# Decoder step on one core: v tiles beside the convolution taps, paired 64-row index scores between v tiles

## What is computed

```python
z = rms_norm(x, norm_g) @ w_in              # q, k, v, gates, index q (8 heads x 64), index k (64), index w (8), GLU
u = glu_a * sigmoid(glu_b)                  # then causal depthwise convolution of width 31 over u
s = einsum('thd,ld->thl', qi, ki) * 64**-0.5
score = einsum('th,thl->tl', wi * 8**-0.5, relu(s)); score = where(k_pos <= q_pos, score, -inf)
_, idx = top_k(score, 256)                  # the 256 best keys of each row are attended
```

## Time and profile before

| | us |
|---|---|
| median of 3 runs | 1038.33 |
| lowest and highest | 1038.2, 1040.77 |
| the profiled execution | 1040.58 |
| its span from first to last instruction | 1038.8 |
| PE busy | 930.8 (90%) |
| DVE busy | 694.0 (67%) |
| ACT busy | 372.5 (36%) |

### The profile page before, as it was taken

How to read it: one execution, slowest core, us unless ns; L and a number is a source line. 1 busy time by engine, 2 the same in 40 slices (tenths; PEclk the granted TensorE clock), 3 DMA queues, 4 the chain that set the end, 5 groups by cost and what they waited for, 6 DMA issues and landing times.

```text
span 1038.8 us, 11317 instructions
## 1 busy us (share of the span) xinstructions
PE 930.8 (90%) x3900; PEld 514.4 (50%) x3900; DVE 694.0 (67%) x1598; ACT 372.5 (36%) x830; POOL 85.4 (8%) x90
## 2 busy tenths in 40 slices
PE   3999999936899999999998899697598789999998
PEld 2866666713243444666643334353366555445432
DVE  5309987999896765888878889966487565432111
ACT  6310101102666656889700000122765364221000
POOL 0211010000541000000000000001011101310000
PEclk9999999877999999999999899788699789999999
DMA  8363020200662302001030000005012102320211
GB/s 291 108 188 62 1 81 3 83 0 1 203 210 83 112 34 84 26 22 61 0 102 21 21 20 12 0 1 210 21 52 61 31 11 62 104 100 31 71 62 42
DMA packets 35314, 69.82 MB, mean 67 GB/s; under 512 B 9609, under 2 KB 11953, under 8 KB 35249
## 3 DMA queue, kind: packets, MB, share of 16 engines
q1 hardware_dynamic: 28089, 43.93, 13.0%
q0 software_dynamic: 7168, 25.17, 7.4%
HBM read 58.46 MB, written 11.11 MB: 67 GB/s over the span
## 4 chain that ended last, share of the span: by engine, by line
PE 72%; DVE 21%; ACT 3%; issue 3%; DMA 1%; SPq 1%; DVEq 0%; ACTq 0%
PE ps L491 67%; DVE ctmp L1267 8%; PE ps L494 4%; DVE ct L1241 1%; DMA xn<-in_x_prompt 1%; DVE pv L1469 1%; ACT PTs L942 1%; ACT uT L1120 1%; DVE LB L1470 1%; DVE mcum L1395 0%; DVE zN L1493 0%; ACT relu L1058 0%; DVE pv L1435 0%; DVE uT L1675 0%; ACT sqj L955 0%
## 5 line engine op out<-in xcount | busy, mean ns | idle before, releaser
L491 PE MATMUL ps<-xT,W 128*128 128x344 f32 x960 | 283.8, 458 | 0.0
L491 PEld LDWEIGHTS ps<-xT,W 128*128 128x128 f32 x960 | 184.0, 193 | 97.6 <-issue 5.6
L491 PE MATMUL ps<-W,xT 128*128 128x512 f32 (+3 forms) x576 | 214.7, 531 | 1.2 <-ACT relu L1058 1.2
L1267 DVE SCALAR_TENSOR_TENSOR ctmp<-uT,chw,ctmp 128x1024 f32<-128x1024 f32 x116 | 152.0, 1310 | 4.1
L491 PEld LDWEIGHTS ps<-W,xT 128*128 128x128 f32 (+1 forms) x576 | 94.9, 185 | 113.7 <-issue 113.3
L1088 ACT ACTIVATE sgj<-SC,candn 128x1024 bf16<-128x1024 f32 (+3 forms) x128 | 114.5, 897 | 8.8 <-DVE candn L1373 6.6
L942 ACT ACTIVATE PTs<-ps 128x512 f32<-128x512 f32 (+3 forms) x96 | 43.1, 484 | 125.7 <-PE ps L494 125.7
L1706 DVE TENSOR_TENSOR ps<-ps,TP 128x256 f32<-128x256 f32 (+1 forms) x64 | 26.4, 412 | 71.2 <-PE ps L491 70.8
L1133 ACT ACTIVATE nsq<-ps 128x512 f32<-128x512 f32 (+1 forms) x18 | 10.7, 596 | 164.5 <-DVE nss L1482 120.9
L491 PE MATMUL ps<-kiT,qz 128*128 128x512 f32 (+3 forms) x160 | 61.7, 530 | 7.6 <-ACT relu L1058 6.5
L494 PE MATMUL ps<-Cc,Pm 128*128 128x128 f32 x288 | 46.6, 303 | 17.7 <-ACT PTs L942 17.5
(11 more groups left out here) (308 smaller groups left out, 1046.4 us busy)
## 6 DMA issues: line engine op xcount, KB each, us to landing
W<-in_w_in SPq DMA_DIRECT2D x8, 2048.0 KB, 8.7
xn<-in_x_prompt SPq DMA_DIRECT2D x8, 512.0 KB, 8.2
W<-in_w_out SPq DMA_DIRECT2D x1, 4096.0 KB, 13.3
resid<-in_x_prompt SPq DMA_DIRECT2D x16, 256.0 KB
out<-resid SPq DMA_DIRECT2D x16, 256.0 KB
out<-V SPq DMA_DIRECT2D x8, 256.0 KB
out<-zN SPq DMA_DIRECT2D x8, 256.0 KB, 2.0
bias_rows<-tprow SPq DMA_DIRECT2D x1, 1536.0 KB
```

The lines of the kernel that those rows point to most:

```text
L491: return nc.tensor.matmul(out, lhsT, rhs, start=start, stop=stop)
L1267: ins = vec.scalar_tensor_tensor(conv[:, c, :] if j == CW - 1 else acc_, src, chw[:, c, j:j + 1], acc_, ALU.mult, ALU.add)
```

## The change

1. `own_score` on PE moves from the tenth qi piece to behind the first v tile. On DVE the own score's operations move ahead by 16 taps, and line 1300 comes 12 taps after them. `decode_u` moves back by 12 taps.
2. The 48 steps become 40 chunks of up to 512 keys and two heads (80 units). PE multiplies rows 0 to 63 and rows 64 to 127 straight from qiT and kiT into two banks (b2 to b5 by turns); `qz` and its copies go. relu has four buffers of 512, in the place of TP, whose load moves in SPq to after the last chunk.
3. The 8 full v tiles are made before the search: five beside the taps (with cached turns 0 and 1), three in slots 5 to 7, each with some ten chunks and two cached turns, half of the chunks in the middle of the tile. The last block's 8 chunks (slot 8) and the sample rows' v tile come last. ACT drains them there, so the search's rounds drain only ga and gc.
4. The cached scores use one bank (b6), and the 1 x 1 matmul (line 638) behind each turn goes. The second sc16 buffer lies where the last block's scores go, so DVE waits in front of that block for the last score DMA (`scd_out[1]`).

```diff
+    CHUNKS = [(i, hp, a) for i in range(2, NT) for hp in range(H // 2) for a in range(0, (i + 1) * P, 512)]
+    FIRST_SLOT, SLOTS = 5, NT + 1
+    CACHED_AT = {1: (0,), 4: (1,), 5: (2, 3), 6: (4, 5), 7: (6, 7)}
+    EVACUATED_EARLY = NT + 1
     def evacuated_after(r):
-        return min(len(DURING_SEARCH), (r + 1) * 33 // 32)
+        return min(len(DURING_SEARCH), EVACUATED_EARLY + r + 1)
@@ PE
-            if j == 9:
-                own_score()
+        def index_scores(n):
+            i, hp, a = CHUNKS[n]
...
+            for e in range(2):
+                begin(("ix", n, e), f"b{2 + 2 * (n % 2) + e}")
+            for e in range(2):
+                r = slice(64 * e, 64 * e + 64)
+                mm(pt(("ix", n, e))[:, 0:width(n)], qiT[r, hp, i * P:(i + 1) * P], kiT[r, a:a + width(n)]).then_inc(plan.fill_sem(("ix", n, e)), 1)
+        for s in range(SLOTS):
+            one, two = halves(s)
...
+            if s < NT:
+                natural("v", s, 2, between)
+            else:
+                between()
+            if s == 0:
+                own_score()
+            for n in cached_in(s)[:1]:
+                cached(n)
+            for n in two:
+                index_scores(n)
+            for n in cached_in(s)[1:]:
+                cached(n)
+        natural("v", NT, 2)
@@ ACT
+        def index_relu(n):
+            for e in range(2):
...
+                if u >= 4:
+                    act.wait_ge(relu_used, u - 3)
@@ DVE
-        taps(0, CW + 24)
+        taps(0, 2 * CW + 5)
...
-        taps(CW + 24, NTAP - 12)
+        taps(2 * CW + 5, NTAP - 28)
...
+        taps(NTAP - 28, NTAP - 16)
         v.wait_ge(*plan.full("sn"))
...
-        taps(NTAP - 12, NTAP)
+        taps(NTAP - 16, NTAP - 8)
+        cached_turn(1)
+        taps(NTAP - 8, NTAP)
+            if (i, hp, a) == (NT - 1, 0, 0):
+                v.wait_ge(scd_out[1], 128)
```

More of the change, by code:

```diff
@@ L526, in natural @@
             rows = P if t < NT else NB
-            o = begin(("z", g, t), f"b{ring[0] % 4}")
+            o = begin(("z", g, t), f"b{ring[0] % banks}")
             ring[0] += 1
             for k in range(KC):
+                if between and k == KC // 2:
+                    between()
                 last = mm(o[0:rows, 0:n], xT[:, k, t * P:t * P + rows], W[:, gi % 2, k, 0:n], k == 0, k == KC - 1)
@@ L1080, in evacuate @@
                 piece_out(g, m, gcT[:, m // 3, a:a + n], sT[:, 3], ACT.Silu)
-        ev = 0
+        for s in range(SLOTS):
+            one, two = halves(s)
+            for n in one:
+                index_relu(n)
+            if s < NT:
+                evacuate("v", s)
+            for n in cached_in(s)[:1]:
+                cached_out(n)
+            for n in two:
+                index_relu(n)
+            for n in cached_in(s)[1:]:
+                cached_out(n)
+        evacuate("v", NT)
+        ev = EVACUATED_EARLY
         for r in range(BITS + 1):
@@ L1777, in _ @@
         for i in range(2, NT):
-            g.wait_ge(relu_used, (i - 1) * H)
+            g.wait_ge(relu_used, 2 * sum(1 for x in CHUNKS if x[0] <= i))
             d = sc(i)[:, i * P:(i + 1) * P]
```

136 lines of the change are left out of this document (63 added, 73 removed).

## The result

The changed kernel takes **1032.87 us** (median of 7 runs) where the kernel before, run beside it on the same chip, takes 1040.77: a ratio of 0.9923, 95% interval 0.9897 to 0.9948. It is faster by 7.9 us, under 1%, and a ratio of 1 lies outside the interval. The forecast was 12.3 us faster, from a median of 1038.33. The profiled execution took 1031.74 us with a span of 1029.9; the forecast's span would have been 1038.8 - 12.3 = 1026.5.

A forecast was written before the change was run, and what follows sets the result against it. PE was taken to bound 346.40 to 547.37 us, nearly tied with DVE. Line 1410 starts 13.3 us earlier, less 1.0 for PE's clock: 12.3 us faster, 1038.33 to 1026.0 us; range 1018 to 1037, own forecast 1018 to 1031.

The forecast's parts named there:

- the case 1031 to 1035.2: Whole kernel: partly lower clock or longer waits would leave the time at 1031 to 1035.2 us; chance 0.13.
- a search that starts after 365 us: Start of the search, forecast near 358 us; a start after 365 us was named as showing the forecast wrong.
- Which engine bounds the search, and the ties there: Search: without v tiles thirty rounds take 4.59 us each, and line 1410 starts directly behind the first norm, 13.3 us earlier.
- The taps: Ahead of the index stage: the 8.11 us glua wait goes (gain 8.1), an own-score wait of 6.1 comes; net 2.7 us.
- When the next turn may start: Index stage, ahead of turn 2: DVE waits for PE's reads of cached turn 1, 258.3 to 262.4 us (4.1 us).
- Small waits for PE at the cached turns add about 1.1: Blocks 2 to 6, turns 3 to 7: waits for PE add about 1.1 us to 68.0; block 6 ends at 338.8.
- The last score DMA: Ahead of the last block: DVE waits 5.5 us, until 344.3, for the last score DMA, which takes 4.8 us.
- The clock loss behind the search: Behind the search: PE's idle of 30 us lowers its clock and costs at most another 1 us.
- first rival: Index scores: pairs don't overlap, index stage 12.7 us later, result 1038.7; chance 0.11 shared with waits that eat the gain.
- The second rival: Blocks from slot 5: PE at 1.2 GHz gives 1043.8 us (slower: 0.09, shared); a third of blocks costs 5 to 8.
- The rounds did shorten: Search, rival: ACT's counts and drains set the first ten rounds, 19.5 us gain missing, 1045; slower 0.09, shared.
- waits that eat the gain: Index stage: waits use up the gain, time within 1035.2 to 1041.4 us; chance 0.11, shared with pairs in series.

The follow-up runs named there:

- e2: Changed kernel with all nine v tiles put back behind the index scores and drained in the search's rounds: 1036.64 us, ratio 0.9966 to the kernel before.
- e9: Changed kernel with the chunks of blocks 2 to 6 spread from slot 4 instead of 5, cached turns rearranged: 1021.08 us, ratio 0.9867 to the kernel before.
- e3: Changed kernel with only the decode u operation back at its old place, 12 taps sooner: 1032.64 us, ratio 0.9925 to the kernel before.
- e6: Changed kernel with DVE's second cached turn of slots 5 to 7 put behind three chunks of the second half: 1036.78 us, ratio 0.9969 to before.
- e4: Changed kernel with PE making the own score ahead of the first v tile: 1032.95 us, ratio 0.9959 to the kernel before.
- e1: Changed kernel with each pair of index matmuls done twice into the same bank: 1041.44 us, ratio 1.0011 to the kernel before.
- e10: Changed kernel with the edits of e9 and e7 together: 1020.15 us, ratio 0.9791 to the kernel before.
- e11: Changed kernel with the edits of e9, e7 and e4 together: 1017.03 us, ratio 0.9760 to the kernel before.
- e5: Changed kernel with the second sc16 buffer in the KV buffer, so DVE skips the last score DMA's wait: 1033.96 us, ratio 0.9915 to before.
- e7: Changed kernel with ACT draining the sample rows' v tile after round 0's counts: 1034.22 us, ratio 0.9944 to the kernel before.
- e12: The same code as e9, measured again: 1020.46 us, ratio 0.9802 to the kernel before.

## Why the prediction was right, and where it was off

*How right.* The 7.9 us lie inside the stated range (1018 to 1037), but not inside what the prediction called its own forecast, 1018 to 1031: it is the case 1031 to 1035.2, to which it gave 0.13. One of its own signs of being wrong came true, a search that starts after 365 us (365.57). And the number was helped by something that no term foresaw: the stretch behind the choice operation was 2.4 us shorter than before, where the sum had it 1.0 longer. That is luck; with the sum's own figure for that stretch the kernel would have taken about 1035 us, still inside the range.

*Which engine bounds the search, and the ties there: right.* Rounds of 4.60 us on average, PE's idle time of 29.3 us behind it, and the choice operation directly behind the norm came as written. From the first candidate to the last it took 138.1 us (forecast 139.4), from there to the choice operation 29.6 (29.9). The table load fell into round 1 (378.30 - 373.19 = 5.1 us) and cost 0.5 us of the 0.75 foreseen. e2 takes the v tiles back and brings back the slow rounds and the wait for PE. What it does not bear out is the size: the sum booked the whole gain to the search, and e2 has 5.4 of the 6.5 us at the choice operation with v where it was. The sum has no term for that: it never asks when PE's chain would start with the paired scores alone. Whether e9's 12 us need v where the change puts it, no run shows either.

*The taps: right in place, sizes off, without effect.* The decode u wait went. The own score's wait was 3.83 us, not 6.1: DVE came to it at 228.1 and not at 226.4 (1.1 of it because its first tap began at 80.17 and not at 79.03), PE's answer at 231.9 and not at 232.5. The first weighing began at 269.33, forecast 269.7, because PE's row, which the forecast had right to 0.4 us, sets it. e3 shows that this, and not the taps, is the reason: with the 8.11 us wait back, its first weighing is 1.0 us later, as is PE's row. The "gain 8.1" was no gain of the kernel.

*When the next turn may start: the step that failed.* The forecast let DVE go on when PE had read the first quarter of the turn before (wait 4.1 us until 262.4). PE goes through the turn's 16 instructions in 1.94 us with its four groups of 32 columns side by side, and the four end together: DVE was released at 263.55, at the end of the turn (261.53 + 1.94 = 263.47), after 6.10 us. Ahead of turn 2 this cost 1.1 us and the first weighing hid it.

*"Small waits for PE at the cached turns add about 1.1": the term that was most mis-sized.* There were 2.40 + 2.44 + 0.47 + 0.84 + 2.75 = 8.9 us, 7.6 of them ahead of turns 3, 5 and 7. Each of these three waits until PE is through half a tile (3.7 us) and the whole turn behind it; that they wait for the whole turn and not for its first quarter is the step above, by an estimate 3 x 1.46 = 4.4 of the 7.6 us (1.46 is three quarters of 1.94). The work itself was 1.6 us less than summed (66.4 for 68.0), so block 6 ended at 344.68 instead of 338.8; relative to the first weighing that is 6.3 us late. e6 shows that this change of DVE's order doesn't dodge the waits, e9 that PE's order does.

*The last score DMA: 7.43 us for 5.5.* The DMA path itself was as forecast (SPq, the issue to all back, with the DVE operation behind it):

```profile
346.87 2.80 SPq L1913 DMA_DIRECT2D decode_scores<-sc16b  x4
352.15 0.35 SPq L1916 DMA_DIRECT2D SD<-decode_scores  x1
```

5.3 us here, 4.8 in the earlier trace rows; but PE took 3.24 us for turn 7's 16 instructions, at a lower clock, where the sum had 1.94. In e4, where they took 1.94, the wait was 5.67 us, nearly the 5.5 of the forecast. Together: -0.4 at the first weighing, +6.3 in the blocks, +1.9 at the DMA, -0.2 in the last block make the search start at 365.57 and not at 358.0, 7.6 us late, which reached the choice operation as 6.8.

*The clock loss behind the search: none there.* The forecast took 1.0 us off for PE's idle time. The tile behind it took 8.76 us where the earlier trace rows has 8.81, so no price was left to pay at that place (both are partly at the lower level only; a tile wholly at 1.2 GHz would take some 13.8 us, an estimate of twice the 6.90, so the prediction's "at most another 1 us" was no bound); the stretch from the choice operation to the end was 489.0 us, 2.4 shorter than before's 491.4. The granted clock by stretch (the first figures behind the window are us; PEclk is third from the right):

```profile
262.00:345.00 83.00, 70.36 (x302) 24.46 (x294) 65.74 (x88) 39.99 (x89) 23.25 (x27) 0.96 0.40 130
345.00:362.00 17.00, 12.76 (x37) 4.24 (x38) 8.74 (x13) 9.13 (x18) 0.11 (x1) 0.80 0.45 143
500.00:530.00 30.00, 6.49 (x16) 2.55 (x14) 27.03 (x102) 12.49 (x29) 0.00 (x0) 0.67 0.00 0
```

*The rivals.* The pairs overlap (first rival out, by the rows of PE and e1). The second rival, a lower clock in the blocks, came in a mild form. Over 83 us of the blocks the clock was 0.96 of full speed, and the missing part lies in two places of some 3.4 us each at the lower level, 1.2 GHz (two rows of windows and two of the timeline of PE):

```profile
312.00:314.00 2.00, 2.00 (x12) 0.32 (x12) 1.71 (x3) 1.02 (x3) 0.00 (x0) 0.56 1.00 352
340.00:342.00 2.00, 2.00 (x12) 0.46 (x14) 1.69 (x4) 1.47 (x3) 0.00 (x0) 0.50 0.04 8
```

```profile
313.04 3.20 PE L512 MATMUL ps<-ct,Qb 128*32 128x512 f32 x16
340.27 3.24 PE L512 MATMUL ps<-ct,Qb 128*32 128x512 f32 x16
```

Turns 5 and 7 took 1.3 us longer each than the other six. Just ahead of them PE had waited 1.51 and 1.37 us, and 2.10 and 0.21. A third place lies in the last 17 us, around the wait for the score DMA, where the clock was 0.80: the 16 instructions behind an idle time of 3.68 us at 354.29 took 6.53 us in place of 2 x 1.99. The rule that stood beside this rival (the Trainium skill, "TensorE: Matmul & The Clock Gate", section "A second HAM failure mode: psum-queue depth-cycling") holds in part here: PE's waits for ACT in the blocks were 0.2 to 2.1 us long, and the clock swung, but in two places only, for 6.8 us of the 83 and not for the third of the blocks that the rival had priced at 5 to 8 us. What the prediction took from the rows of before, no fall after a wait of 2.35 us, does not carry over; and in e3 the clock fell behind a wait of 1.77 us where in the changed kernel, behind the same wait, it did not. So the length of the last wait alone doesn't decide it.

The rounds did shorten. The case "waits that eat the gain" came nearest: the waits of DVE in the index stage, 13.3 us in the sum, were 6.10 + 1.16 + 8.9 + 7.43 = 23.6.

## What to carry to other kernels

When a long row of work is moved from one engine's overloaded stage into another, draw up both engines' rows in the new place and look for every point where one overwrites what the other still reads; here such a wait lasted to the end of the *whole* group of instructions that read the buffer, with whatever stood ahead of it in that engine's queue. A wait that vanishes on an engine that isn't the bound of its stretch is no term of the sum (here 8.1 us); what counts is the row of the engine that ends the stretch. And where waits remain, try to move work of the engine that is waited for (e9, 12 us faster) before that of the waiting one (e6, 4 us slower). When a change has several parts, take each back by itself: e2 shows that the part meant to bring the gain brought 1.1 of 6.5 us at the place where it was expected.

## What the runs showed of the hardware

**A gain of two or three microseconds can be gone 150 us later.** Behind the choice operation PE and DVE have the same work in all kernels, yet the stretch to attention's first minimum takes either 170.3 to 170.5 us (changed, e1, e3, e6, e10, e11) or 172.5 to 174.6 (before, e2, e4, e5, e7, e9, e12), and the rest 318.3 to 319.7 or 321.6 to 322.9. A norm stage's tile of 16 instructions takes 7.0 to 7.1 us at 2.4 GHz and 8.2 to 10.2 when part of it runs at 1.2 (the changed kernel's tile at 544.43 took 8.76 us, with a granted clock of 0.64 until 549 us and 1.00 behind that); which tiles these are differs. Two rows at the same place in the program, the first of the changed kernel, the second of e9:

```profile
668.74 7.11 PE L512 MATMUL ps<-W,xT 128*128 128x512 f32 x16
```

```profile
654.38 8.81 PE L512 MATMUL ps<-W,xT 128*128 128x512 f32 x16
```

Runs of one and the same kernel differ in the same way: e12's six runs lie at 1019.6 to 1020.6 us with a mean granted clock of 0.941 and at 1024.4 to 1024.8 with 0.937, and three of e5's at 1025.2 to 1026.3 with 0.940 to 0.941 where the other seven lie at 1031.9 to 1035.0 with 0.932 to 0.935. So e5's and e7's 2 us at the choice operation don't reach the end in most runs. It need not be chance each time: nine of e7's ten runs lie at 1033.0 to 1036.3, and a start some microseconds sooner may itself move the places where the clock falls, which isn't shown. Why it falls in one place and not in the other is left open; no run here varied that alone.

**The same holds inside the index stage.** The same 16 instructions behind the same waits took 1.94 or 3.2 to 3.3 us (turn 4 in the changed kernel and in e3 and e5, turn 7 in e4 and in the changed kernel), and that moved the search's start by 1.7 to 1.8 us between kernels whose code behind turn 2 is the same (e3 and e4 against the changed kernel).

**Four groups of 32 columns run side by side and end together.** 16 instructions of 512 columns take 1.94 us, 0.12 each. The next turn's first transpose waits for the first group alone, and yet it starts 0.07 to 0.08 us behind the end of all four, each time that it has to wait (263.55 behind 263.47, 278.46 behind 278.38, 303.60 behind 303.53, 330.81 behind 330.74).
